# A hybrid attention and recurrence block: another order of the first loads, splits and sums

## The reference

```python
h = rmsnorm(x, w_norm_pre)
q_a, k_a, v_a, z_a, q_r, f_r, i_r, z_r = split(h @ w_in)       # widths 512,128,128,512 and 4 x 512
q_a, k_a = rope(q_a), rope(k_a)
o_a = sliding_window_sink_attention(q_a, k_a, v_a, sinks) * silu(z_a)   # chunks of 64, this chunk and the one before
o_r = hgrn2_chunkwise(q_r, f_r, i_r, lb)                       # gated linear recurrence over chunks of 64
o_r = rmsnorm(o_r, hgrn_norm) * silu(z_r)
x = x + rmsnorm(concat([o_a, o_r]) @ w_out, w_norm_post)
```

## Time and profile before

| what | value |
| --- | --- |
| median of 3 runs | 1015.95 us |
| lowest and highest | 1011.29 and 1016.07 us |
| profiled execution, span from first to last instruction | 1012.9 us |
| profiled execution, its own time | not given on the page; the median is 3.05 us above the span |
| PE busy | 955.5 us, 94% of the span |
| DVE, ACT, POOL busy | 599.8, 529.3, 526.9 us |
| granted TensorE clock, mean | 0.985 of full speed |

### The profile page before, as it was taken

The page is one execution under the profiler, slowest core; times in us unless marked ns, Lnnn a source line. Parts: engine busy times, 40 slices in busy tenths (PEclk is TensorE's granted clock), DMA queues, the critical chain, the costliest instruction groups (busy, mean ns, idle before and its releaser), DMA issues.

```text
span 1012.9 us, 14850 instructions
## 1 busy us (share of the span) xinstructions
PE 955.5 (94%) x4656; PEld 761.9 (75%) x4656; DVE 599.8 (59%) x994; ACT 529.3 (52%) x1138; POOL 526.9 (52%) x295
## 2 busy tenths in 40 slices
PE   7898999999999999999989999999999989999996
PEld 4686777778878777778868778777887867777785
DVE  7657775555355866655346776556435577655553
ACT  5136556665224655676341556665642265567553
POOL 3344544962553545575364463676354345548635
PEclk9898999999999999999999999999999999999998
DMA  6362111114545211110556321111255621111132
GB/s 254 112 190 84 63 63 63 63 42 146 210 151 171 84 63 63 63 63 22 208 200 200 109 67 63 64 63 63 84 188 182 204 84 63 63 63 63 42 135 115
DMA packets 31881, 108.71 MB, mean 107 GB/s; under 512 B 4400, under 2 KB 4656, under 8 KB 31280
## 3 DMA queue, kind: packets, MB, share of 16 engines
q1 hardware_dynamic: 24352, 93.33, 26.7%
q10 hardware_dynamic: 7440, 14.30, 4.4%
HBM read 93.99 MB, written 8.39 MB: 101 GB/s over the span
## 4 chain that ended last, share of the span: by engine, by line
issue 42%; POOL 28%; PE 18%; DVE 6%; ACT 4%; DMA 1%; POOLq 0%; DVEq 0%; ACTq 0%
POOL w_lo L981 21%; PE bank L350 9%; PE bank L359 4%; POOL probs L986 2%; DVE f_a L933 2%; POOL k_end L1032 1%; PE bank L413 1%; POOL q_gate L1044 1%; POOL k_dec L1011 1%; POOL x_acc L991 1%; ACT w_hi L529 1%; DMA vec<-in_vectors 1%; PE bank L412 1%; DVE g_a L807 1%; DVE h_mix L853 1%
## 5 line engine op out<-in xcount | busy, mean ns | idle before, releaser
L981 POOL TENSOR_TENSOR w_lo<-w_raw,w_hi 128x1024 fp32r<-128x1024 f32 x137 | 334.1, 2442 | 413.1 <-ACT w_hi L529 413.1
L350 PE MATMUL bank<-h_hi,w_hi 128*128 128x512 f32 x832 | 338.8, 407 | 4.8 <-DVE h_lo L718 3.9
L350 PE MATMUL bank<-h_hi,w_lo 128*128 128x512 f32 x832 | 336.1, 404 | 0.0
L350 PE MATMUL bank<-h_lo,w_hi 128*128 128x512 f32 x832 | 332.3, 399 | 0.0
L529 ACT ACTIVATE w_hi<-w_raw 128x1024 fp32r<-128x1024 f32 x138 | 144.2, 1050 | 163.1 <-PE bank L359 52.9
L350 PEld LDWEIGHTS bank<-h_hi,w_hi 128*128 128x128 f32 x832 | 158.6, 191 | 51.6 <-issue 16.1
L350 PEld LDWEIGHTS bank<-h_hi,w_lo 128*128 128x128 f32 x832 | 158.7, 191 | 28.7 <-issue 1.5
L350 PEld LDWEIGHTS bank<-h_lo,w_hi 128*128 128x128 f32 x832 | 158.3, 190 | 29.1
L359 PE MATMUL bank<-w_lo,mix_hi 128*128 128x512 f32 x256 | 101.3, 396 | 0.0
L359 PE MATMUL bank<-w_hi,mix_hi 128*128 128x512 f32 x256 | 101.1, 395 | 0.0
L359 PE MATMUL bank<-w_hi,mix_lo 128*128 128x512 f32 x256 | 101.0, 395 | 0.0
(11 more groups left out here) (150 smaller groups left out, 1501.3 us busy)
## 6 DMA issues: line engine op xcount, KB each, us to landing
w_raw<-in_weights SPq DMA_DIRECT2D x138, 512.0 KB, 3.3
x_in<-in_x SPq DMA_DIRECT2D x4, 2048.0 KB, 11.3
x_in<-in_x_rows SPq DMA_DIRECT2D x8, 1024.0 KB, 4.9
out<-q_gate ACTq DMA_DIRECT2D x12, 512.0 KB, 3.2
f_b<-f_a ACTq DMA_DIRECT2D x48, 64.0 KB, 2.0
x_in<-in_x SPq DMA_DIRECT2D x4, 512.0 KB, 7.6
f_d<-f_c ACTq DMA_DIRECT2D x32, 64.0 KB, 3.9
out<-q_gate ACTq DMA_DIRECT2D x8, 256.0 KB, 3.2
```

The costliest lines, as they stand in the source:

```text
L350: mm = pe.matmul(acc(w)[:, :], stationary[:, s, k, :], moving[:, k, :], start=(m == 0), stop=(m == 3 * KT - 1), skip_group_check=True)
L981: pool.tensor_tensor(w_lo[:, s, :, :], w_raw[:, RAW_SLOT[w], :, :], w_hi[:, s, :, :], ALU.subtract).then_inc(lo_split.sem, 1)
```

## The change

It has these parts. (1) SP issues `vec`, first of all, in place of ACT; weight tile 1 is loaded after the first piece of x. (2) ACT splits weight tile 1 after four blocks of x, not after two, and squares all 8 blocks, in order, where it did 6. (3) DVE makes w_lo of tiles 0 and 1, the second between its blocks 3 and 4 of h_lo, and all seven adds of the first sum of squares; POOL makes neither w_lo of tile 1 nor adds. (4) Six fills of state go from DVE to POOL; DVE waits for them before its loop. (5) In every round PE takes steps 0 and 1 together: blocks 0 to 3 of tile 0, then of tile 1, then blocks 4, 5 of each, then 6, 7 of each. (6) In every round the product that sums x_acc is at m == 12 of step 2.

The core of the diff:

```diff
+ENTRY = [(w, k) for part in ((0, 1, 2, 3), (4, 5), (6, 7)) for w in (K_TILE, V_TILE) for k in part]
...
-            for w in range(FIRST_SPLIT):
-                load_weights(0, w)
+            sp.dma_start(vec[:, :], vectors).then_inc(vec_loaded, 16)
+            load_weights(0, 0)
             for k in range(0, KT, 2):
+                if k == 2:
+                    load_weights(0, 1)
                 sp.dma_start(x_in[:, k:k + 2, :], ...).then_inc(x_first[k // 2], 16)
...
-                if m == 0 and w == XSUM:
+                if m == 12 and w == XSUM:
                     sum_x(t)
...
-                for w in range(OUT0):
+                for w, k in ENTRY:
+                        pe.wait_ge(h_lo_done.sem, h_lo_done.after(t, k))
+                        if k == 0:
+                            pe.wait_ge(lo_split.sem, lo_split.after(t, w))
+                            pe.wait_ge(y_read.sem, y_read.after(t, (2, 3)[w] - 8))
+                        for m in range(3 * k, 3 * k + 3):
+                            products(w, m, m == 3 * KT - 1)
+                for w in range(V_TILE + 1, OUT0):
                     pe.wait_ge(lo_split.sem, lo_split.after(t, w))
...
-            act.dma_start(vec[:, :], vectors).then_inc(vec_loaded, 16)
...
-                if k == 0:
-                    for w in range(1, FIRST_SPLIT):
-                        split_hi(0, w)
-            for i, k in enumerate(FIRST_SQUARES):
-                steps = KT - i if i == len(FIRST_SQUARES) - 1 else 1
-                act.activation(q_gate[:, k, :], x_in[:, k, :], ACT.Square).then_inc(x_squared.sem, steps)
+                if k == 2:
+                    split_hi(0, 1)
+            for k in range(KT):
+                act.activation(q_gate[:, k, :], x_in[:, k, :], ACT.Square).then_inc(x_squared.sem, 1)
...
             for k in range(KT):
+                if k in (0, 4):
+                    w = k // 4
+                    dve.wait_ge(hi_split.sem, hi_split.after(0, w))
+                    dve.tensor_tensor(w_lo[:, w, :, :], w_raw[:, w, :, :], w_hi[:, w, :, :], ALU.subtract).then_inc(lo_split.sem, 1)
                 low_h(0, k)
...
+            for k in range(1, KT):
+                dve.wait_ge(x_squared.sem, x_squared.after(0, k))
+                if k > 1:
+                    dve.wait_ge(sum_step, k - 1)
+                dve.tensor_tensor(x_acc[:, :], x_acc[:, :] if k > 1 else q_gate[:, 0, :], q_gate[:, k, :],
+                                  ALU.add).then_inc(*((sum_step, 1) if k < KT - 1 else (x_added.sem, x_added.per_tile)))
...
+            dve.wait_ge(pool_setup, 1)
...
-            pool.wait_ge(lo_split.sem, lo_split.after(0, 0))
-            split_lo(0, 1)
...
+            pool.memset(carry[:, :, :], 0.0)
+            pool.memset(k_t[:, :, :], 0.0)
+            pool.memset(v_t[:, 0:CHUNK], 0.0)
+            pool.memset(a_t[:, :], 0.0)
+            pool.memset(first_mask[:, 0:CHUNK], NEG_INF)
+            pool.memset(first_mask[:, CHUNK:P], 0.0).then_inc(pool_setup, 1)
+            pool.wait_ge(lo_split.sem, lo_split.after(0, 1))
```

More of the change, by code:

```diff
@@ L100 @@
 FIRST_SPLIT = 2
-FIRST_SQUARES = (0, 2, 4, 6, 1, 3)
-FIRST_POOL = 3
 Y_POOL = (0, 2)
@@ L251, in hybrid_block @@
         y_scaled, finished_pool = count("y_scaled", 2), count("finished_pool", 2)
-        pool_sum = sem("pool_sum")
+        pool_setup = sem("pool_setup")
         def loaded(sems, uses, tile, i, n=1):
@@ L456, in _ @@
             with pe.Fori(0, TILES) as t:
-                for w in range(OUT0):
+                for w, k in ENTRY:
[6 more added lines that the diff above has]
+                for w in range(V_TILE + 1, OUT0):
                     pe.wait_ge(lo_split.sem, lo_split.after(t, w))
                     if w < 3:
-                        pe.wait_ge(y_read.sem, y_read.after(t, (2, 3, 1)[w] - 8))
+                        pe.wait_ge(y_read.sem, y_read.after(t, 1 - 8))
                     else:
@@ L464, in _ @@
                     for m in range(3 * KT):
-                        if w == 0 and m % 3 == 0:
-                            pe.wait_ge(h_lo_done.sem, h_lo_done.after(t, m // 3))
                         between(t, w, m)
@@ L991, in add_x @@
                 pool.tensor_tensor(x_acc[:, :], x_acc[:, :], x_sq[:, :], ALU.add).then_inc(x_added.sem, 1)
-            pool.wait_ge(lo_split.sem, lo_split.after(0, 0))
-            split_lo(0, 1)
-            for i in range(1, FIRST_POOL):
-                pool.wait_ge(x_squared.sem, x_squared.after(0, i))
-                if i > 1:
-                    pool.wait_ge(pool_sum, i - 1)
-                pool.tensor_tensor(x_sq[:, :], x_sq[:, :] if i > 1 else q_gate[:, FIRST_SQUARES[0], :],
-                                   q_gate[:, FIRST_SQUARES[i], :], ALU.add).then_inc(pool_sum, 1)
+            pool.memset(carry[:, :, :], 0.0)
[5 more added lines that the diff above has]
+            pool.wait_ge(lo_split.sem, lo_split.after(0, 1))
             with pool.Fori(0, TILES) as t:
```

## The result

| | before | after |
|---|---|---|
| time, median (range), us | 1014.65 (1011.29 to 1016.07) | 1023.24 (1022.21 to 1024.37) |
| span of the profiled execution, us | 1012.9 | 1022.3 |
| mean granted clock of PE | 0.985 | 0.977 |
| PE busy, us | 955.5 | 961.8 |
| PE idle (span less busy), us | 57.4 | 60.5 |

The changed kernel takes 1.0091 times the time of the kernel before, with the interval 1.0071 to 1.0111: 8.6 us slower by the medians, 9.4 us by the spans. The median before is now that of four runs; the prediction had three of them, with 1015.95. The forecast was 1018.8, that is 2.8 us slower, a change too small to tell. The time lies inside the range, near the rival with long stretches of half clock (1025.5), but the change is three times the one forecast.

What follows compares the result with a forecast made beforehand. PE, 94% busy, was taken as bound by a slackless chain from x_scale to the turned probabilities. Entry -9.2, late sum +8.6, clock +3.4 gave +2.8 on 1012.9, so 1015.7; plus 3.05 carried for the median, 1018.8 us; range 1006 to 1026.

Steps and rivals of the forecast that it cites:

- the rival with long stretches of half clock: Step 10 of tiles 1 to 3: idle time brings 6.8 us stretches, 3.4 lost per round; +9.6, 1025.5 us; chance 0.3.
- PE's entry: Tile 0: step 2 starts at 23.1, the sum ends and x_scale starts at 27.0, 9.2 us earlier.
- The adds: Entry, DVE: seven adds at 0.69 follow the squares, ending at 19.7 before POOL's first split at 20.2.
- From the sum to x_scale: Tile 0: x_scale starts as the sum ends, at 27.0, where it was 36.19.
- The fills: Six fills on POOL at the entry: nothing; at most DVE's first split is held 3.1 us, hidden behind PE's matmuls.
- that half of the rule which the prediction names: Skill's rule: two-input VectorE instructions don't block against GpSimd instructions that only write SBUF, so the fills hold up nothing.
- The late sum in later rounds: Step 2, tiles 1 to 3: late x_scale delays PE's turn by 3.4, 3.4, 1.8 us; 8.6 in all, between 5.4 and 10.
- The clock: Behind steps 9 and 10: one more 3.4 us half-clock stretch in tiles 1 and 2 each; +3.4 us, bounds 0 and 10.2.
- A sign that misled: PE's wait for probabilities at step 10 near 5 us; under 2.5 in tiles 1 to 3 means a time near 1007.
- The blocks: Steps 0 and 1 by blocks, later rounds: the 48 products end at the same time, K copied 4.1 us later; nothing.
- The entry doesn't deliver: Rival, tile 0: adds and splits still meet, or w_lo of tile 2 comes at 27; 1021 to 1026 us, chance 0.05.

Runs made afterwards that it cites:

- few adds: Changed kernel with only three of the seven adds of the first tile's sum of squares, blocks 4 to 7 left out: 1017.42 us, ratio 1.0026.
- the kernel with fillers: Changed kernel plus 16 products per tile with overwritten results (11 and 5), in PE's idle time at step 10: 1014.41 us, ratio 0.9991.
- the sum ahead of the wait: Changed kernel with the sum of squares ahead of PE's wait for w_lo of tile 2: 1015.34 us, ratio 1.0005.
- the late load: Changed kernel with the 2 MB load of the next x issued behind weight tile 13, not 10: 1016.85 us, ratio 1.001.

## Why the prediction was wrong

Step by step, with what the traces show:

- *PE's entry.* Right. Step 2 was forecast at 23.1 and started at 23.32; POOL's first split at 20.2, and it was 20.66. The loads were a little worse (piece 1 of x rounded at 10.63, not 9.7), inside the bound.
- *The adds. This is the step that failed:* "The seven adds at 0.69 follow the squares and end at 19.7, before POOL's first split starts at 20.2". To end at 19.7, seven adds of 0.69 would have had to start at 14.9, when DVE was still making h_lo. They start at 17.08, behind h_lo and three small operations, and go at 0.80 from start to start. So even alone they would end near 22.6, and the last two met splits, up to 26.5. I had left out what stands ahead of the first add (2.2 us), and the gap between an add and the next one that needs it (0.7 us over seven). The gain at the turn was 3.2 us of 9.2. With few adds x_scale stood at 27.07, which shows the rest of the entry right.
- *From the sum to x_scale.* I put x_scale right behind the sum. The small operations, the copy of K and ACT's swaps stand ahead of it, and once the adds are late these are too. This step wasn't in my sum, though the earlier trace rows show 4.9 us there already; half of what the sum's product had won was lost in it.
- *The fills.* Right at nothing. The two largest took 0.53 and 1.06 us, at 2 us, long before anything could wait for them. DVE's first split started at 5.88, when all fills were done, so no run here shows whether a fill would have held it up; that half of the rule which the prediction names, on instructions that only write, stays untested.
- *The late sum in later rounds.* Right in place and nearly in size. x_scale 3.8 us later behind step 2 in tile 1 (forecast 3.85) and 4.2 in tiles 2 and 3, 8.36 us from there to the copy (forecast 8.34), the same 40 us on to the turn, and the turn 3.5, 3.0 and 3.5 us later (forecast 3.4, 3.4, 1.8). Tile 3 was undersized: I took full clock there, as before, but in the changed kernel that step 2 begins at half clock too. At full clock, as in the kernel with fillers, it was 2.2.
- *The clock.* Right in total, forecast +3.4, measured +2.6 by the table (-0.7, +1.5, +1.45, +0.3), but by luck, for its parts were not right. I gave tiles 1 and 2 one new stretch of 3.4 us each and left tiles 0 and 3 as they were; tiles 1 to 3 got 6.83 and tile 0 10.24. But each began 2.6 to 5 us before the turn, where PE is waiting in the chain anyway, so that only what lies behind the turn was lost.
- *A sign that misled.* I wrote that PE's wait for the probabilities at step 10 would be near 5 us, and that under 2.5 us in tiles 1 to 3 would mean a time near 1007. It was 1.80, 1.56 and 1.12 us, and the time was not near 1007. The idle time fell on two waits: 2.64, 2.34 and 2.82 us more were spent just ahead, at the scores.
- *The blocks.* Right at nothing: ratio 1.0000.

So the forecast's sum, -9.2 + 8.6 + 3.4 = +2.8, came out as -3.2 + 10.0 + 2.6 = +9.4. Of the 6.6 us between them the entry has 6.0.

The rival with long stretches came close to the time, and the 6.8 us stretch did come in each of the three rounds, but its sum was not what happened. It had the full entry, -9.2, and 10.2 for the clock. The trace has 6 us less gain from the first and 7.6 less loss from the second, and 1.4 more from the late sum; that the errors nearly cancel is luck. The rival "The entry doesn't deliver", with x_scale in tile 0 behind 31 and 1021 to 1026 us, to which I gave 0.05, named the step that failed, and the place: "adds and splits still meet". It deserved more, since the margin between the adds' end and the first split was 0.5 us, less than the error of either figure.

What stays open: why an idle time ahead of step 2 brings half clock in one round and not in another. Tile 3 of the kernel before kept full clock with 2.35 us, and so did tiles 2 and 3 of the change without its late sum with 2.69 and 2.74, while the kernel with fillers fell to half clock with 2.13 and 2.31. The length of the idle time alone does not tell. That K's swap ahead of x_scale costs time was argued from the order of the rows; no run moved it alone. And whether the sum at some product between 0 and 12 does better than at 0 was not tried.

## What to carry to other kernels

A wait that is removed at the entry is removed once; an order written into a loop is paid in each round, so read the same place in a later round before counting a gain. When two operations must not meet and the sum leaves 0.5 us between them, price the case in which they do, and count dependent instructions from start to start, from the time at which the engine is free. An operation of VectorE that is moved, earlier or later, has to be read against what GpSimd does at its new place; and of a stretch at half clock only the part counts in which TensorE itself sets the time.

## What the hardware did that I had not expected

- While PE had work left, half clock came in stretches of 3.41, 6.83 or 10.24 us. In the changed kernel, idle time of PE of 2.5 to 2.8 us ahead of a step 2 was followed by 3.41 each time, and two idles of 2.64 and 1.80 us, with a short group of scores between them, by 6.83. But like idles did not always bring like stretches: 3.91 and 1.09 us brought 10.24 in tile 0 of the changed kernel, 3.94 and 1.09 brought 6.83 with the sum ahead of the wait, and about 1.0 and 2.1 brought 6.83 in two tiles and 3.41 in another with the late load. Products whose results nobody reads, in the idle time around the scores, kept the clock at 1.00 there and gave back 8.8 us of 1023.
- A VectorE instruction on 128x4 values took 2.33 us beside a split of POOL, against 0.16 for its neighbours of the same size, the row at 29.06: what is paid there is the other engine's instruction, not one's own size. The Trainium skill ("SBUF — State Buffer", Who interferes with whom) says that the two block each other in full when VectorE reads two inputs from SBUF and GpSimd reads it too. The trace agrees, for an instruction that starts behind a split's start: 2.3 to 2.9 us beside splits of 2.4 to 2.8 us, and 1.08 where only the end of a split was met, at 285.95 in the kernel before. One that starts ahead of the split is not held up: the add at 20.25 took 0.69, with the split starting at 20.66.
- Fills on POOL are cheap beside its splits: 0.53 us for 512 columns and 1.06 for 1152, where the split's pace would give 1.4 and 3.1.
- Dependent adds of VectorE go at 0.80 us from start to start, against 0.69 in a row's duration.
- Four small swaps behind a 2 MB load on another queue made DVE wait 7.3 us; with the load later it was 1.25.
